# Finishing a token inside the expert loop of a mixture-of-experts step, at the later of its two slots

## The reference

```
probs = softmax(x1 @ w_router)                       # 16 experts, 4 groups of 4
gate  = top 2 experts of the best group, weights normed to 1
h = silu(x1 @ w_gate[e]) * (x1 @ w_up[e])            # width 256
y = sum over the token's two experts of gate[e] * (h @ w_down[e])
out = layer_norm(ALPHA * x1 + y) * g + b             # ALPHA = 2 ** 0.25
```

## Time and profile before

| | us |
|---|---|
| median of 3 runs | 1246.33 |
| lowest to highest | 1239.85 to 1248.85 |
| the profiled execution, its own time | 1243.51 |
| its span | 1241.7 |
| TensorE busy in the span | 1108.9 (89%) |
| VectorE, ScalarE, GpSimd busy | 415.6, 316.4, 82.3 |

### The profile page before, as it was taken

How to read it: one execution, slowest core, us unless ns; L and a number is a source line. 1 busy time by engine, 2 the same in 40 slices (tenths; PEclk the granted TensorE clock), 3 DMA queues, 4 the chain that set the end, 5 groups by cost and what they waited for, 6 DMA issues and landing times.

```text
span 1241.7 us, 14170 instructions
## 1 busy us (share of the span) xinstructions
PE 1108.9 (89%) x4690; PEld 594.3 (48%) x4691; DVE 415.6 (33%) x900; ACT 316.4 (25%) x633; POOL 82.3 (7%) x124
## 2 busy tenths in 40 slices
PE   7999999999999979999998899992799999999800
PEld 6646755444455434446455455552444444444400
DVE  2112434346534531431344233247111111111178
ACT  0101323555211155443322020110111111111143
POOL 3100000000000010000000000000110110011062
PEclk9999999999988879999998999995699999999955
DMA  8302020502000031115507251114587697775283
GB/s 240 90 21 65 2 68 1 164 1 52 1 1 0 3 81 52 35 43 32 173 1 261 81 173 65 68 43 144 197 312 252 201 370 265 264 272 186 98 309 122
DMA packets 109642, 149.23 MB, mean 120 GB/s; under 512 B 23994, under 2 KB 82682, under 8 KB 109562
## 3 DMA queue, kind: packets, MB, share of 16 engines
q1 hardware_dynamic: 92858, 112.63, 28.6%
q0 software_dynamic: 6464, 22.56, 5.2%
q10 hardware_dynamic: 10272, 13.40, 2.9%
HBM read 118.50 MB, written 32.02 MB: 121 GB/s over the span
## 4 chain that ended last, share of the span: by engine, by line
PE 83%; DVE 8%; DMA 3%; SPq 2%; issue 2%; ACT 1%; POOL 0%; POOLq 0%; ACTq 0%; DVEq 0%
PE psum_all L1363 18%; PE psum_all L1952 13%; PE psum_all L1872 9%; PE psum_all L1479 8%; PE psum_all L1940 7%; PE psum_all L1434 4%; PE psum_all L1510 3%; PE psum_all L1544 3%; PE psum_all L1923 2%; PE psum_all L1568 2%; DVE arena L2643 1%; PE psum_all L1536 1%; PE psum_all L1507 1%; DMA arena<-x_scratch,tok_now 1%; PE psum_all L1832 1%
## 5 line engine op out<-in xcount | busy, mean ns | idle before, releaser
L1363 PE MATMUL psum_all<-arena 128*128 128x512 f32 (+7 forms) x800 | 231.9, 461 | 0.0
L1952 PE MATMUL psum_all<-arena 128*128 x400 | 177.4, 597 | 2.3 <-DMA arena<-in_w_exp_down 1.4
L1363 PEld LDWEIGHTS psum_all<-arena 128*128 128x128 f32 (+1 forms) x800 | 129.1, 180 | 89.0 <-issue 63.2
L1872 PE MATMUL psum_all<-arena 128*128 128x512 f32 (+1 forms) x288 | 118.4, 593 | 0.0
L1952 PEld LDWEIGHTS psum_all<-arena 128*128 128x128 f32 x400 | 74.6, 192 | 87.5 <-issue 87.5
L1479 PE MATMUL psum_all<-arena 128*128 128x512 f32 (+1 forms) x288 | 104.3, 518 | 0.0
L1065 ACT ACTIVATE psum_all<-psum_all,neg_max 128x128 f32<-128x128 f32 (+7 forms) x96 | 65.6, 683 | 141.5 <-DVE neg_max L2084 141.2
L1940 PE MATMUL psum_all<-arena 128*128 x200 | 90.2, 593 | 0.9 <-ACT arena L1307 0.9
L1872 PEld LDWEIGHTS psum_all<-arena 128*128 128x128 f32 (+1 forms) x288 | 50.2, 184 | 61.6 <-issue 61.6
L1479 PEld LDWEIGHTS psum_all<-arena 128*128 128x128 f32 x288 | 49.4, 201 | 51.5 <-issue 51.2
L2620 DVE SCALAR_TENSOR_TENSOR arena<-psum_all,slot_gate,arena 128x256 f32<-128x256 f32 x25 | 12.1, 484 | 176.7 <-ACT arena L1302 176.7
(11 more groups left out here) (390 smaller groups left out, 1197.7 us busy)
## 6 DMA issues: line engine op xcount, KB each, us to landing
arena<-in_w_exp_gate SPq DMA_DIRECT2D x16, 1024.0 KB, 8.4
arena<-in_w_exp_up SPq DMA_DIRECT2D x16, 1024.0 KB, 11.0
arena<-in_w_exp_down SPq DMA_DIRECT2D x16, 1024.0 KB, 13.1
slot_rows<-arena ACTq DMA_DIRECT2D x25, 512.0 KB, 5.6
arena<-in_x_prompt SPq DMA_DIRECT2D x16, 512.0 KB, 3.7
arena<-in_cache_fox_kv SPq DMA_DIRECT2D x32, 256.0 KB, 3.1
arena<-in_w_in SPq DMA_DIRECT2D x2, 2048.0 KB, 8.8
arena<-in_cache_nsa_kv SPq DMA_DIRECT2D x64, 64.0 KB, 1.8
```

Source lines behind the costliest of these rows:

```text
L1363: ins = nc.tensor.matmul(row_bank(j)[p0:p0 + n, 0:cn], xT[:, k, tok0(t):tok0(t) + n], wv[:, k, c0:c0 + cn], start=(k == 0), stop=(k == KD ...
L1872: ins = nc.tensor.matmul(psum[2 * (t % 2) + i][p0:p0 + n, :], lhs, wo[:, k, i * 512:(i + 1) * 512], start=(k == 0), stop=(k == KD - 1), ti ...
L1952: ins = nc.tensor.matmul(psum[0][:], xT_slot[:, k, :], arena[:, bass.ds(w_at + k * 2 * F, 2 * F)], start=(k == 0), stop=(k == KD - 1))
```

## The change

A token is finished as soon as the second of its two slots is computed, inside the expert loop.

- For each slot, `partner_of` holds the row of the token's other slot where that one lies earlier, and `row_of` the token's output row. A slot whose other slot lies later, and a slot that holds no token, gets any row as partner (a row of slot tile 0) and one of 128 spare output rows. No row is left out of a gather or a store. The output for prompt and sample is one array of 1088 + 128 rows.
- The lists come from a second set of 18 matrix products on TensorE (into `psum[7]`), and from ten small operations on VectorE (`find_partners`).
- In the loop, for each tile: ScalarE makes ALPHA times the gathered x rows (`scale_x`, four buffers); GpSimd gathers the partner rows (`gather_partner`); two tiles later VectorE adds both (`add_rows`) and ScalarE takes the square and the square root (`square`), and loads the function table for silu again with a one-column operation; VectorE normalizes (`normalize`); GpSimd stores the rows with an indirect DMA (`store_finished`).
- The gather of the next x rows now also waits for `scale_x` (`ax_ready`), since it overwrites `x_slot`.
- Everything behind the loop is gone but for the last two tiles' finish. The zeros for unused slot tiles are no longer stored in the loop: all of `slot_rows` is cleared much earlier, by nine DMAs on ScalarE's queue during the projections, the first from SBUF, eight from DRAM to DRAM (2 MB each).
- Experts 2 and 3 are loaded when `indices_ready` is set, as the lists lie where their weights go.

```
+                if N_ROWJ + i in CLEAR_AFTER:          (and in the row groups)
+                    clear_slot_rows(CLEAR_AFTER[N_ROWJ + i])
+            def clear_slot_rows(c):
+                if c == 0:
+                    act.wait_ge(pool_step, 4)
+                    zeros = zeros_bf[:].bitcast(F32).unsqueeze(1).to_broadcast([P, 2 * D // P, P // 2])
+                    act.dma_start(y_dram[0].rearrange("p (i n) -> p i n", n=P // 2), zeros).then_inc(slots_cleared, 16)
+                    return
+                act.wait_ge(slots_cleared, 16)
+                act.dma_start(y_dram[4 * c - 3:4 * c + 1].rearrange("s p d -> p s d"),
+                              y_dram[0].unsqueeze(1).to_broadcast([P, 4, D])).then_inc(slots_cleared, 16)
...
 SyncE
             sp.wait_ge(slots_ready, 1)
             sp.wait_ge(xs_in, 16)
+            sp.wait_ge(indices_ready, 1)
             load_expert(sp, 2, 2)
             load_expert(sp, 3, 3)
-            with sp.Fori(last_tile(sp) + 1, NSL) as t:
-                sp.dma_start(y_dram[bass.ds(t, 1)].rearrange("s p d -> (s p) d"), no_rows[:]).then_inc(rest_cleared, 16)
...
 GpSimd
+            def gather_partner(col, n, used):
+                if used is not None:
+                    pool.wait_ge(partner_used, used)
+                pool.tensor_copy(partner_now[:], partner_of[:, col]).then_inc(partner_set, 1)
+                pool.wait_ge(indices_ready, 1)
+                pool.wait_ge(ys_stored, stored)
+                pool.wait_ge(partner_set, n)
+                pool.indirect_dma_start(partner_rows[:], None, slot_rows,
+                                        bass.IndirectOffsetOnAxis(ap=partner_now[:], axis=0)).then_inc(partner_in, 16)
+            def store_finished(col, n):
+                pool.wait_ge(out_ready, n)
+                pool.tensor_copy(row_now[:], row_of[:, col]).then_inc(row_set, 1)
+                pool.wait_ge(row_set, n)
+                pool.indirect_dma_start(y_rows, bass.IndirectOffsetOnAxis(ap=row_now[:], axis=0), out_row[:], None
+                                        ).then_inc(y_stored, 16)
+            def next_x(t):
+                pool.wait_ge(xs_turned, t * 2 + 2)
+                pool.wait_ge(ax_ready, t + 1)
+                gather_x1(bass.ds(t + 1, 1), t + 2 if isinstance(t, int) else pool.to_reg(t + 2))
+            with pool.Fori(1, last - 2) as n:
+                next_x(n + 3)
+                gather_partner(bass.ds(n + 1, 1), n + 1, n)
+                store_finished(bass.ds(n, 1), n)
...
 ScalarE
+            def scale_x(t, freed):
+                act.wait_ge(xs_in, t * 16 + 16)
+                if freed is not None:
+                    act.wait_ge(z_done, freed)
+                nc.scalar.activation(scaled_x(t), x_slot[:], ACT.Copy, scale=ALPHA).then_inc(ax_ready, 1)
+            def square(t):
+                nc.scalar.activation(squares[:], scaled_x(t), ACT.Square, bias=fin_s[:, 1:2],
+                                     accum_out=fin_s[:, 2:3]).then_inc(fin_squared, 1)
+                act.wait_ge(fin_squared, t)
+                nc.scalar.activation(fin_s[:, 2:3], fin_s[:, 2:3], ACT.Sqrt, bias=lnc[:, 0:1], scale=1.0 / D
+                                     ).then_inc(fin_std, 1)
+                nc.scalar.activation(fin_s[:, 4:5], lnc[:, 0:1], ACT.Silu)
             def slot_tile(t, before, finish, freed):
                 act.wait_ge(hid_done, t + 1)
                 nc.scalar.activation(sil[:], psum[0][:, 0:F], ACT.Silu).then_inc(sil_ready, 1)
                 copy_x(t * 2 + 4)
+                scale_x(t + 1, freed)
+                if done:
+                    act.wait_ge(fin_mean, finish)
                 if some:
-                    copy_rows(t, before * 16)
+                    copy_rows(before)
                 act.wait_ge(h_turned, t + 1)
                 nc.scalar.copy(h_T[:].rearrange("p f n -> p (f n)"), psum[6][:, 0:F]).then_inc(hT_ready, 1)
                 if some:
                     store_rows(t)
+                if done:
+                    square(finish)
...
 TensorE, before the loop
+            pe.wait_ge(hots_ready, 2)
+            for j in range(TOP_K * TILES):
+                ins = nc.tensor.matmul(psum[7][:, 0:NSL], lo_hot[:, j, :], partner_vals[:, j, :],
+                                       start=(j == 0), stop=(j == TOP_K * TILES - 1))
...
 VectorE
+            def find_partners():
+                dve.wait_ge(slots_done, 2)
+                (ten operations of 1 to 33 columns; the last sets indices_ready)
+            def add_rows(t):
+                A = scaled_x(t)
+                dve.wait_ge(partner_in, t * 16)
+                dve.wait_ge(ax_ready, t + 1)
+                V.tensor_tensor(A, A, partner_rows[:], ALU.add).then_inc(partner_used, 1)
+                dve.wait_ge(y_act, t + 1)
+                dve.wait_ge(y_dve, t + 1)
+                V.scalar_tensor_tensor(out=A, in0=A, scalar=1.0, in1=y_slot[:], op0=ALU.mult, op1=ALU.add,
+                                       accum_out=fin_s[:, 0:1]).then_inc(fin_summed, 1)
+                V.tensor_scalar(fin_s[:, 1:2], fin_s[:, 0:1], -1.0 / D, None, ALU.mult).then_inc(fin_mean, 1)
+            def normalize(t, before):
+                V.scalar_tensor_tensor(out=z_row[:], in0=scaled_x(t), scalar=fin_s[:, 1:2], in1=ln_row[1][:, 0, :],
+                                       op0=ALU.add, op1=ALU.mult).then_inc(z_done, 1)
+                dve.wait_ge(fin_std, t)
+                V.reciprocal(fin_s[:, 3:4], fin_s[:, 2:3]).then_inc(fin_rstd, 1)
+                if before is not None:
+                    dve.wait_ge(y_stored, before * 16)
+                V.scalar_tensor_tensor(out=out_row[:], in0=z_row[:], scalar=fin_s[:, 3:4], in1=ln_row[1][:, 1, :],
+                                       op0=ALU.mult, op1=ALU.add).then_inc(out_ready, 1)
             def slot_tile(t, before, finish, stored):
                 (product of silu, up part and gate, as before)
                 copy_x(t * 2 + 3)
+                if finish is not None:
+                    add_rows(finish)
+                if before is not None:
+                    copy_rows(before)
+                if finish is not None:
+                    normalize(finish, stored)
+            with dve.Fori(1, before2) as m:
+                slot_tile(m + 3, m + 2, m + 1, m)
+            add_rows(before)
+            copy_rows(last)
+            normalize(before, before2)
+            add_rows(last)
+            normalize(last, before)
```

More of the change, by code:

```diff
@@ L1034, in _ @@
-            for t in range(1, TILES, 2):
-                n = rows_of[t]
-                v = layer[0:n, t, :]
-                pool.wait_ge(gained, t + 1)
-                pool.tensor_tensor(v, v, ln_row[1][0:n, 1, :], ALU.add).then_inc(odd_normed, 1)
         @block.scalar
```

255 lines of the change are left out of this document (134 added, 121 removed).

## The result

The changed kernel took 1230.46 us, the median of 4 runs (1222.6 to 1234.45), beside 1247.46 us (1239.85 to 1248.85, 4 runs) for the kernel before. The ratio is 0.9871, with a 95% interval of 0.9823 to 0.992: faster by 17 us (1.3%), a little over half of the 31 us that the forecast of 1215 stood for. The profiled execution took 1229.79 us with a span of 1228.0 us, which is 13.7 us less than the span before.

What follows compares the result with a forecast made beforehand. The prediction took TensorE to bound the loop. From the span of 1241.7 it took 43.8 for the end and added 4 (start), 1 (clears) and 8 (loop): 1210.9; plus 1.8 and 2.8 to the median, 1215. Range 1199 to 1240.

Steps and rivals of the forecast that it cites:

- the dense stretch is bound by DMA and more: Rival, expert loop: x gathers 2 us late in most expert-loading tiles, 27 us more; time 1234.5, chance 0.18.
- the prediction named as its sign: In the loop: TensorE's idle time ahead of L1923 or L1952 summing to over 25 us or nothing would refute the prediction.
- Bound of the loop: Expert loop: TensorE bounds it, busy for all 11.39 us of a tile.
- Start of the loop, 4 us: Loop start: second product set, list operations and later gathers cost 4 us, ends 0 and 7.
- Clears, 1 us: Projections: issuing nine clearing DMAs on ScalarE costs 1 us, ends 0 and 5.
- The loop, 8 us: Steady loop: about 12 of 23 tiles have x gathers 0.7 us late beside expert loads; 8 us, ends 0 and 25.
- The ceiling of "about 365 GB/s": DMA throughout: about 365 GB/s is all that the 16 engines give, from a tile at 363 GB/s.
- The finish in the loop: Each loop tile: added ScalarE and VectorE work is done at S + 10.3 (S: silu's start), at no cost.
- The end, 43.8 us: Behind the loop: only the last two tiles' finish remains, ending at 1197.9 in place of 1241.7, a gain of 43.8 us.
- The queue's pace: Rival, loop: three row transfers a tile in GpSimd's queue take 14.6 us against 11.39; time 1281, chance 0.09.
- little contention: Rival, loop and its start: together they cost 3 us or less; time 1205.5, chance 0.20.

Runs made afterwards that it cites:

- run 1: Changed kernel, but loading only one eighth of the weights of experts 4 to 15; loop 274.13 us, against 293.5 in the changed kernel.
- run 2: Changed kernel with the gather of partner rows replaced by a plain load of 128 x 64 elements; loop 284.2 us.
- run 10: Changed kernel with earlier token gathers, skipped rows and SyncE waiting at the end, plus GpSimd awaiting next tokens before the partner gather; median 1242.74 us.
- run 3: Changed kernel with the scattered store of finished tiles replaced by a plain store of 128 x 64 elements to spare rows; loop 294.3 us.
- run 4: Changed kernel with the last finished tile stored by SyncE as a plain transfer to spare rows; 31.2 us behind the last silu, against 39.8.
- run 7: Changed kernel with the wait for the last scattered store moved from GpSimd to SyncE; 36.6 us behind the last silu, against 39.8.

## Why the prediction was wrong

The direction and the mechanism held: the work behind the loop went into the free time of VectorE and ScalarE, and the price was paid in late gathers. The time, 1230.5, lies inside the range and outside the forecast's own (1208 to 1225); it is nearest to the rival "the dense stretch is bound by DMA and more" (1234.5). Two terms of the sum were mis-sized, one in the loop and one at the end. The idle time ahead of the two groups of products that the prediction named as its sign stayed under its 25 us: 13.0 us ahead of L2000 and 3.2 ahead of L2029.

- **Bound of the loop: held.** In tiles without expert loads TensorE is busy for all of 11.40 us.
- **Start of the loop, 4 us: mostly absent.** The first silu came 0.1 us later than before; the second tile took 13.4 instead of 12.0 us. That is 1.5 us in all, of which only the second tile's 1.4 is clear of the spread, as run 1 has it too.
- **Clears, 1 us: not to be told.** The same 0.1 us covers them in this pair, and in a stage that spreads from 885.2 to 899.5 us neither 1 us nor none can be read.
- **The loop, 8 us: the first failed step.** "About 12 of 23 tiles have their x gather wholly beside expert loads, at 0.7 us late each." The start was right: S + 3.6 forecast, 1059.02 - 1055.48 = 3.54 measured. The landing was not: 7.95 us was taken from the earlier trace rows, from a gather beside experts alone, and here seven gathers took 8.2 to 9.8 us. The trace of the kernel before had the whole spread, if not this end of it: 4.2 us at best, 5.9 in the median, 8.1 at most. Each further microsecond falls entirely on TensorE, since the slack was already spent. Why the slowest became slower is not settled: without the partner's bytes (run 2) it was still 9.2, and with no partner gather in flight (run 10) 9.8. The gather leaves 1.6 us later than before (3.6 us behind the silu instead of 2.0) and so runs longer beside ScalarE's store and the weights, which no run took apart. Two things were left out: a late partner gather makes ScalarE late, and so the next token gather (the chain above), and the granted clock falls behind a stall. Together they made 20.8 - 1.4 = 19.4 us out of 8. Run 1 shows that all of it hangs on the experts' traffic, run 2 that about half of it goes with the partner gather's bytes.
- **The ceiling of "about 365 GB/s": too low.** Tiles at 400 GB/s and stretches at 408 are in the trace of the changed kernel, and the trace of the kernel before already had more than 365, in a tile of the loop and behind it:

```profile
911.00:922.40 11.40, 11.40 (x35) 5.56 (x34) 1.77 (x3) 1.83 (x4) 1.15 (x2) 1.00 1.03 392
...
1202.50:1207.50 5.00, 0.00 (x0) 0.00 (x0) 4.90 (x8) 3.17 (x7) 4.42 (x3) 0.50 1.03 420
```

The row of 363 was one tile of several, not the densest. By the average there was room all along (0.83 of the DMA time, 301 GB/s). The forecast's step from the sum of bytes to lateness was a weak argument: run 3 took 0.5 MB off each tile and gained nothing.

- **The finish in the loop: held.** ScalarE and VectorE are through at S + 10.4 in a tile without a stall, 10.3 forecast. Table loads took 1.28 us and nothing more: ScalarE's root starts right behind (1213.15 + 1.28 = 1214.43, root at 1214.45). The drain of 1.38 us on top that the Trainium skill has in "ScalarE: Activation LUTs", section "What ACT_TABLE_LOAD costs", does not show in this trace.
- **The end, 43.8 us: the second failed step.** "End: 1197.9" was S + 30.7 of the last tile, and the span ended at S + 39.8, 9.1 us later. The terms: from the landing of the last store to the end of the span 7.2, nearly all of it GpSimd's closing (a DRAIN of 6.77), which the forecast put at nothing; it stands in the trace of before, hidden beside SyncE's stores; the last partner gather 2.3, which came behind a store on GpSimd whose index copy and build took 1.26 and 1.37 us instead of 0.18 and 0.98; small gaps between the steps of the last two finishes 0.8; and on the other side the scattered store, which landed 3.3 us behind the start of its issue instead of "I take 4.5".
- **Rivals.** The queue's pace (1281) and little contention (1205.5) fell. In the rival of the dense stretch the pieces were there (x gather late by 2 us, finish of two tiles before delayed) with 32 us of cost against the full 43.8 of gain; measured were 20.9 and 34.6. That its time was near is luck: 11 us too much cost in the loop and 9 us too much gain at the end cancelled.

## What to carry to other kernels

Before adding a transfer to a loop, ask what waits for it and what it delays, and not only how many bytes the loop moves: taking a scattered store of 0.5 MB off each tile gave nothing here, taking a gather of the same size off gave 9 us. Read the landing times of all gathers from the trace before, with their spread, and not only the two in the chain. Work moved into a loop of a bound engine is paid at its thinnest slack, and a stall there costs more than itself where the clock falls. And look at which engine ends the program, in the sequencer's records too: the 7 us of an end on GpSimd were in both traces here and were paid only where GpSimd was the last.

## What was not expected of the hardware

- GpSimd ends with a DRAIN: 6.7 to 6.8 us in the kernel before, the changed kernel and run 4, and 7.7 us where it begins beside the last issue (run 7). From GpSimd's last issue to the end of the span lie 7.0 to 7.1 us if GpSimd waits for nothing; the landing comes on top if it does (8.4 to 9.6 us). With SyncE last, the span ended within 1 us of the last bytes.
- GpSimd's copy of 128 numbers took 0.18 us alone and up to 1.3 us beside a VectorE operation with two SBUF inputs, ending with it in 31 of 32 cases. GpSimd's build of an indirect transfer took up to 2.0 us; the shortest took 0.96.
- The DMA engines moved 400 to 408 GB/s in dense windows of the changed kernel, and 392 and 420 in two windows of the kernel before, not the 365 that one tile had suggested.
- Indirect transfers that skip about two thirds of their rows by a bounds check took no longer to build (1.04 us each for the partner gathers), used as many packets with 16 MB less in them, and shortened the loop by 12.8 us.
